# A fused encoder layer on one core: when the second block of each MLP pass adds its first tile, and what the down product of the last 32 rows waits for

## The chip, the core and the metric

The kernel runs on one core of a Trainium2 chip. A core has TensorE (matrix products), VectorE, ScalarE and GpSimd (work on whole tiles), and SyncE, which here issues most transfers. Each engine works through its own list of instructions in order, and they meet only at semaphores. The metric is the device time of one execution in microseconds, the median of three runs. In profile lines PE is TensorE, PEld its loading of weights, DVE is VectorE, ACT ScalarE, POOL GpSimd, SP or SPq SyncE's queue.

## The reference, cut to what matters

One layer of a streaming encoder: a mixer (mLSTM heads and windowed attention), an MLP, and a gated per-layer embedding with a final norm. It is computed for 2048 prompt rows and for 32 sample rows, all in float32 with a width of 1024. The change touches only the MLP:

```
x = x + jnp.square(jax.nn.relu(_rmsnorm(x, g_mlp) @ w_up)) @ w_down
```

with w_up of 1024 x 4096 and w_down of 4096 x 1024.

## The kernel before, in words

**Stages.** The mixer's work fills the first 950 us or so of the span. The MLP follows in three passes over the rows, and then the embedding's stage. The rows are 16 tiles of 128 (numbers 0 to 15) and a last one of 32 rows (number 16, called `NT`). The first pass has six tiles, the second five, the third six: the 32 last rows, and then tiles 11, 12, 15, 13, 14, in this order.

**Blocks.** Each pass goes through 16 blocks of hidden columns (`BLOCKS`), 256 columns a block. In block b TensorE first makes the up product, as seven products of half size in the manner of Strassen (`up`, L2238), and then the down product of the block before (`down(p, b - 1)`, L2291). The first block of a pass has no down product, the second has its first, and in the last block of the third pass the down products of block 14 and of block 15 come one behind the other, with the turning of the next stage's first tile between them ("drained" in `body` of `tensor`). Block 0, block 1 and the last block are written out; blocks 2 to 14 are a loop (`blocks`, L1906).

**High and low parts.** A float32 product is made of three products of rounded values (`split_product`, L107): every operand is split into a high part, made by ScalarE, and a low part, made by VectorE from the operand and its high part. For the up weights of a block there are seven such pairs: `up_weight_hi` (L2073) and `up_weight_lo` (L2367). Four of the seven weights are sums of quarters of the raw weights. `add_weights` (L2359) makes three of these sums on VectorE once the block's raw weights have landed, a fourth one stands behind the first low part (L2374). ScalarE's first high part needs the third sum. For the down weights there are two pairs (`down_weight_hi`, L2084, `down_weight_lo`, L2376).

**The down product.** `down` takes one tile after another into two accumulation banks in turn (`down_ps[n % 2]`; in the profile `m_turned` for even n and `m_proj` for odd n). A tile of 128 rows is 12 matmuls of 512 columns. Tile n waits until tile n - 2 has been added to the rows' running sum, which VectorE does in `add` (L2425, L2439), and the first two tiles wait for the low parts of the down weights. The 32 last rows are another case: their product is taken from the raw weights and an unsplit operand (L2305, 4 float32 matmuls, which the profile shows as 8), in four quarters of the bank's rows; their first add in a pass is a copy (L2431). They are the first tile (n = 0) of the third pass, and before their product TensorE waited for the two high parts of the down weights.

**VectorE's order in a block.** In blocks 1 to 14 it makes, in `body` of `vector` from L2564 on: the two low parts of the down weights (in block 1 they are made between the steps of `chain`), the combining and squaring of the seven products (`chain`, L2441), then `add_weights` for the next block, and then the adds, with the low parts of the next block's up weights between them. How many stand behind which add is said by `shared`: four of the seven in front of the middle of the tiles, the other three behind it. In the first two passes that is two behind the first add and two behind the second; in the third pass it is two, one and one.

**ScalarE's order.** In a block: its copy of the first product, the two high parts of the down weights, four high parts of the next block's up weights, two quarters of the hidden values, three more high parts, two more quarters (L2205 to L2213).

**SyncE's order.** The raw up weights of the block after next are asked for when all seven low parts of the next block are made (L1995), the raw down weights after their low parts are made and, in the third pass, after the last rows' product of the block before is done (L2000 to L2004).

Of the kernel before, what the change touches and what calls it, by code (L numbers as in the profile page):

```python
# [46 lines left out]
def reached(eng, sem, count):  # L47

    if isinstance(count, int) and count <= 0:
        return  # L50
    eng.wait_ge(sem, count)
# [1599 lines left out]
def mlp_programs(nc, ctx, m, a, x_mid, hx_kept, up_kept, w_up, w_down, x_mlp):  # L1651
# [59 lines left out]
    def tiles(p):  # L1711
        pairs = [unit for unit in UNITS[p] if len(unit) == 2]
        halved = [unit[0] for unit in UNITS[p] if len(unit) == 1]
        return [i for i in halved if i == NT] + [a for a, _ in pairs] + [i for i in halved if i != NT] + [b for _, b in pairs]

    def side0_done(p):
        return len(tiles(p)) - 1 - sum(len(unit) == 2 for unit in UNITS[p])
# [23 lines left out]
    def block_count(p, b):  # L1741
        return b + p * BLOCKS

    def made_count(p, b):
        return b + p * (BLOCKS - 1)
# [472 lines left out]
    def tensor(pe, rest):  # L2218
# [72 lines left out]
        def down(p, b):  # L2291
            k = last_group(p, b)
            w_hi, w_lo = down_hi, down_lo
            u_high, u_rest = u_split(p, b)
            for n, i in enumerate(tiles(p)):
                if i == NT:
                    reached(pe, u_hi, u_count(p, k) + 4)
                    reached(pe, down_hi_made, block_count(p, b) * 2 + 2)
                else:
                    reached(pe, u_lo, u_count(p, k) + (2 if place(p, i)[1] == 0 else 4))  # L2300
                reached(pe, added, added_count(p, b, n - 2 if n >= 2 else -1))
                if i == NT:
                    for piece in range(4):
                        f, c = piece // 2, piece % 2
                        ins = pe.matmul(down_ps[n % 2][piece * DEC:(piece + 1) * DEC, 0:NB], u_dec[:, f, :],  # L2305
                                        down_raw[:, f, c * NB:(c + 1) * NB], start=True, stop=True)
                    ins.then_inc(down_done, 1)
                    continue
                for f in (0, 1):
                    if n < 2:  # L2310
                        reached(pe, down_lo_made, block_count(p, b) * 2 + 1 + f)
                    for c in range(D // NB):
                        cols = slice(c * NB, (c + 1) * NB)
                        ins = split_product(pe, down_ps[n % 2][0:tokens(i), cols],
                                            (lambda f: stationary(u_high, f, p, i), lambda f: stationary(u_rest, f, p, i)),
                                            (lambda f: w_hi[:, f, cols], lambda f: w_lo[:, f, cols]), [f], f == 0, f == 1)
                ins.then_inc(down_done, 1)
# [19 lines left out]
    def vector(dve, rest, then):  # L2337
# [21 lines left out]
        def add_weights(g):  # L2359
            a11, a21, a22 = up_raw[:, 0, 0:HC], up_raw[:, 1, 0:HC], up_raw[:, 1, HC:KC]  # L2360
            reached(dve, up_in, g * 32 + 32)
            dve.tensor_tensor(sums_sb[:, 0], a21, a22, ALU.add).then_inc(sums, 1)
            dve.tensor_tensor(a21, a11, a21, ALU.subtract).then_inc(sums, 1)
            reached(dve, sums, g * 4 + 1)
            dve.tensor_tensor(sums_sb[:, 1], sums_sb[:, 0], a11, ALU.subtract).then_inc(sums, 1)  # L2365
# [59 lines left out]
        def add(p, b, n, i):  # L2425
            reached(dve, down_done, down_count(p, b, n))
            if i == NT:
                total, new = acc[:, n, 0:NB], down_ps[n % 2][:, 0:NB]
                if is_block(b, 0):
                    dve.wait_ge(acc_out, 16 * sum(len(tiles(m)) for m in range(p)))  # L2430
                    dve.tensor_copy(total, new).then_inc(added, 1)  # L2431
                    return
            else:
                total, new = acc[0:tokens(i), n, :], down_ps[n % 2][0:tokens(i), :]
                if is_block(b, 0):
                    dve.wait_ge(acc_in, acc_loaded(p))
            if not is_block(b, 0):
                reached(dve, added, added_count(p, b - 1, n))
            dve.tensor_tensor(total, total, new, ALU.add).then_inc(added, 1)  # L2439
# [100 lines left out]
        for p in PASSES:  # L2540
            def body(b):
                first, last = is_block(b, 0), is_block(b, BLOCKS - 1)
                if first and p == 0:
                    k, cols = group_count(p, b), all_cols(p)
                    ahead = second(p)
                    chain(k, cols.stop - cols.start, ahead)
                    for _ in range(3):
                        next(ahead)
                    for n in range(4):
                        u_low(p, b, k, cols, n)  # L2550
                    whole(ahead)
                    return
                if first:
                    for u, cols in enumerate(groups(p, b)):
                        k, w = group_count(p, b) + u, cols.stop - cols.start
                        ahead = second(p)
                        chain(k, w, ahead)
                        for _ in range(3):
                            next(ahead)
                        for n in range(4):  # L2560
                            u_low(p, b, k, cols, n)
                        whole(ahead)
                    return
                k, cols = group_count(p, b), all_cols(p)  # L2564
                if not is_block(b, 1):
                    for f in (0, 1):
                        down_weight_lo(p, b - 1, f)
                chain(k, cols.stop - cols.start, last_down_lo(p, b) if drains(p, b) else first_down_lo(p) if is_block(b, 1) else iter(()))
                if drains(p, b):
                    ahead, made = ready_pass(p + 1), 0  # L2570
                    for n, i in enumerate(tiles(p)):
                        for _ in range(lows_before(n) - made):
                            next(ahead, None)
                        made = lows_before(n)
                        u_tile_lo(p, k, n, i)
                        if n:
                            for _ in range(2):
                                next(ahead, None)
                            made += 2
                            add_drained(p, n - 1, tiles(p)[n - 1])  # L2580
                    whole(ahead)
                    add_drained(p, n, i)
                    yield
                    return
                if last:
                    for n, i in enumerate(tiles(p)):
                        add(p, b - 1, n, i)
                        if n == 0:
                            for m in range(4):
                                u_low(p, b, k, cols, m)  # L2590
                        for _ in range(ITEMS_BEFORE[n]):
                            next(then)
                    for f in (0, 1):
                        down_weight_lo(p, b, f)
                    for n, i in enumerate(tiles(p)):
                        add(p, b, n, i)
                        for _ in range(ITEMS_BESIDE[n]):
                            next(then, None)
                    whole(then)
                    yield  # L2600
                    return
                add_weights(made_count(p, b) + 1)
                ahead = ready(p, b + 1)
                half, count = side0_done(p), len(tiles(p))
                for n, i in enumerate(tiles(p)):
                    add(p, b - 1, n, i)
                    if n < half:
                        items = shared(4, half, n)
                    elif n > half:
                        items = shared(3, count - 1 - half, n - half - 1)  # L2610
                    else:
                        items = 0
                        for m in (0, 1):
                            u_low(p, b, k, cols, m)
                    for _ in range(items):
                        next(ahead, None)
                for m in (2, 3):
                    u_low(p, b, k, cols, m)
                yield

            whole(blocks(dve, p, body))
# [439 lines left out]
```

## Time and profile before

| | |
|---|---|
| time, median of 3 runs | 2599.46 us (2599.33 to 2600.07) |
| the profiled execution's own time | 2600.81 us |
| its span, first to last instruction | 2599.2 us |
| TensorE busy | 2558.8 us, 98% |
| VectorE busy | 1884.8 us, 73% |
| ScalarE busy | 905.1 us, 35% |
| mean granted TensorE clock | 0.996 |
| second block of the three passes, its down product | from 1012, 1503 and 1922 us |
| last two down products of the MLP | from 2320 and 2337 us |

Busy shares are means over the whole span; what a wait is worth is read at its place. In the rows below a line has the start, the duration, the engine, the line of the kernel, the operation, what is written and what is read, and in square brackets the idle time of the engine before it and whose work ended it. Matmuls overlap: the next one starts about 0.23 us after the one before, while a single one is shown with 0.39 us.

### The profile page before, as it was taken

To read this page: it belongs to the slowest core of one execution; us is meant where nothing else is said; L and a number is where in the kernel's file an instruction comes from. 1 tells how busy PE (TensorE), PEld (TensorE's weight loads), DVE (VectorE), ACT (ScalarE), POOL (GpSimd) and SP (SyncE) were. 2 spreads that over 40 slices of the span, in tenths; PEclk is the share of its full clock that TensorE was granted. 3 is DMA by queue.
4 is the path that set the end of the run, shared out by engine and by line. 5 is a ranking of instruction groups with operands and counts; after the bars stand their busy time and mean duration, and the time that the engine had idled before them with its cause. 6 is when DMAs were issued, how large, how long until landed. Compare 5 with 4: busy or idle time off the path is not lost.

```text
span 2599.2 us, 40780 instructions
## 1 busy us (share of the span) xinstructions
PE 2558.8 (98%) x14143; PEld 2224.1 (86%) x14143; DVE 1884.8 (73%) x3281; ACT 905.1 (35%) x2097; POOL 78.7 (3%) x170
## 2 busy tenths in 40 slices
PE   8999999999999999999999999999999999999999
PEld 6888888878888878999999888989888888888887
DVE  7777777775555568777777788888887887885443
ACT  5333333454444443222222323232332332343322
POOL 0000000000000000000000000000000000000010
PEclk9999999999999999999999999999999999999999
DMA  5112111542232336222222542323342222233223
GB/s 211 58 57 85 56 56 51 178 156 98 105 109 97 112 129 236 65 65 65 65 65 65 196 136 65 97 65 97 121 156 81 65 80 65 81 142 135 86 73 108
DMA packets 163367, 261.86 MB, mean 101 GB/s; under 512 B 11440, under 2 KB 111256, under 8 KB 162520
## 3 DMA queue, kind: packets, MB, share of 16 engines
q1 hardware_dynamic: 160936, 252.29, 28.9%
q0 software_dynamic: 2352, 8.52, 1.0%
q8 instruction: 49, 0.80, 0.1%
q14 instruction: 30, 0.25, 0.0%
HBM read 199.99 MB, written 60.62 MB: 100 GB/s over the span
## 4 chain that ended last, share of the span: by engine, by line
PE 89%; DVE 6%; issue 2%; ACT 1%; DMA 1%; POOL 0%; ACTq 0%; DVEq 0%; SPq 0%; POOLq 0%
PE m_proj L112 12%; PE m_proj L114 12%; PE m_proj L113 12%; PE m_turned L112 6%; PE m_turned L114 6%; PE m_turned L113 6%; PE m_acc L114 5%; PE m_acc L112 5%; PE m_acc L113 5%; PE m_pair L113 4%; PE m_pair L112 4%; PE m_pair L114 4%; PE m_pair L1260 1%; PE m_turned L1268 1%; PE m_acc L1285 1%
## 5 line engine op out<-in xcount | busy, mean ns | idle before, releaser
L2082 ACT ACTIVATE f_up_hi<-f_sums 128x512 fp32r<-128x512 f32 x138 | 85.8, 621 | 507.1 <-DVE f_sums L2365 489.8
L2396 DVE TENSOR_TENSOR f_part<-f_part,m_acc 128x384 f32<-128x384 f32 (+2 forms) x240 | 119.2, 513 | 139.9 <-PE m_acc L114 137.1
L112 PE MATMUL m_proj<-f_down_hi,f_uT_hi 128*128 128x512 f32 x476 | 188.9, 397 | 2.5 <-DVE f_acc L2439 2.5
L114 PE MATMUL m_proj<-f_down_hi,f_uT_lo 128*128 128x512 f32 x476 | 185.6, 390 | 0.0
L112 PE MATMUL m_turned<-f_down_hi,f_uT_hi 128*128 128x512 f32 x472 | 183.9, 390 | 1.6 <-DVE f_acc L2431 0.9
L113 PE MATMUL m_proj<-f_down_lo,f_uT_hi 128*128 128x512 f32 x476 | 185.2, 389 | 0.0
L113 PE MATMUL m_turned<-f_down_lo,f_uT_hi 128*128 128x512 f32 x472 | 184.1, 390 | 0.0
L114 PE MATMUL m_turned<-f_down_hi,f_uT_lo 128*128 128x512 f32 x472 | 183.9, 390 | 0.0
L2439 DVE TENSOR_TENSOR f_acc<-f_acc,m_proj 128x1024 f32<-128x1024 f32 x118 | 143.7, 1218 | 45.4 <-PE m_proj L114 45.2
L2439 DVE TENSOR_TENSOR f_acc<-f_acc,m_turned 128x1024 f32<-128x1024 f32 x131 | 151.5, 1156 | 27.6 <-PE m_turned L114 25.5
L2106 ACT ACTIVATE f_uT_hi<-f_part 128x256 fp32r<-128x256 f32 (+2 forms) x300 | 92.3, 364 | 202.0 <-PE m_turned L114 122.2
L2372 DVE TENSOR_TENSOR f_up_lo<-f_up_raw,f_up_hi 128x512 fp32r<-128x512 f32 x184 | 123.2, 683 | 0.0
L112 PEld LDWEIGHTS m_proj<-f_down_hi,f_uT_hi 128*128 128x128 f32 x476 | 89.3, 188 | 38.8 <-issue 13.5
L2378 DVE TENSOR_TENSOR f_down_lo<-f_down_raw,f_down_hi 128x1024 fp32r<-128x1024 f32 x92 | 108.3, 1214 | 0.0
L114 PEld LDWEIGHTS m_proj<-f_down_hi,f_uT_lo 128*128 128x128 f32 x476 | 89.3, 188 | 19.2
L112 PEld LDWEIGHTS m_turned<-f_down_hi,f_uT_hi 128*128 128x128 f32 x472 | 88.6, 188 | 20.0 <-issue 2.4
L2082 ACT ACTIVATE f_up_hi<-f_up_raw 128x512 fp32r<-128x512 f32 x184 | 104.7, 616 | 0.0
L113 PEld LDWEIGHTS m_proj<-f_down_lo,f_uT_hi 128*128 128x128 f32 x476 | 89.4, 188 | 17.8
L114 PEld LDWEIGHTS m_turned<-f_down_hi,f_uT_lo 128*128 128x128 f32 x472 | 88.6, 188 | 18.6
L113 PEld LDWEIGHTS m_turned<-f_down_lo,f_uT_hi 128*128 128x128 f32 x472 | 88.6, 188 | 17.5
L112 PE MATMUL m_proj<-a_wo_hi,a_mixT_hi 128*128 128x512 f32 x256 | 103.1, 403 | 0.0
L2400 DVE SCALAR_TENSOR_TENSOR f_part<-f_part 128x384 f32<-128x384 f32 (+2 forms) x192 | 99.4, 518 | 5.0
(452 smaller groups left out, 7324.8 us busy)
## 6 DMA issues: line engine op xcount, KB each, us to landing
f_down_raw<-in_w_down SPq DMA_DIRECT2D x96, 512.0 KB, 5.1
f_up_raw<-in_w_up SPq DMA_DIRECT2D x92, 512.0 KB, 5.2
hT_hi_kept<-m_hT_hi SPq DMA_DIRECT2D x17, 512.0 KB, 5.0
hT_lo_kept<-m_hT_lo SPq DMA_DIRECT2D x17, 512.0 KB, 5.8
a_hT_hi<-hT_hi_kept SPq DMA_DIRECT2D x17, 512.0 KB, 3.7
a_hT_lo<-hT_lo_kept SPq DMA_DIRECT2D x17, 512.0 KB, 4.6
m_x<-in_x_prompt SPq DMA_DIRECT2D x16, 512.0 KB, 4.2
a_x_sum<-in_x_prompt SPq DMA_DIRECT2D x16, 512.0 KB, 6.2
```

The costliest lines, as they stand in the source:

```text
L112: eng.matmul(out, lh(k), rh(k), start=f, stop=False)
L113: eng.matmul(out, lh(k), rl(k), start=False, stop=False)
L114: ins = eng.matmul(out, ll(k), rh(k), start=False, stop=e)
L1260: ins = pe.matmul(out, head, kT[:, g, 0:slots, :], start=n == 0, stop=n == 1)
L1268: ins = pe.transpose(turned[0:n, p * GRP + h, 0:t.n], s[0:t.n, g, h, p * P:p * P + n], ident[0:t.n, 0:t.n])
L2082: act.activation(up_hi[:, q], weight(q), ACT.Copy).then_inc(up_hi_made, 1)
L2106: ins = act.activation(out, part[PART_OF[quarter]][:, at], ACT.Copy)
L2372: dve.tensor_tensor(up_lo[:, q], weight(q), up_hi[:, q], ALU.subtract).then_inc(up_lo_made, 1)
L2378: dve.tensor_tensor(down_lo[:, f], down_raw[:, f], down_hi[:, f], ALU.subtract).then_inc(down_lo_made, 1)
L2396: dve.tensor_tensor(part[out][:, 0:w], part[other][:, 0:w], up_ps[bank][:, 0:w], ALU.add).then_inc(combined, 1)
L2400: dve.scalar_tensor_tensor(x, x, 0.0, x, ALU.max, ALU.mult).then_inc(squared, 1)
L2439: dve.tensor_tensor(total, total, new, ALU.add).then_inc(added, 1)
```

## The change

Two edits. In the second block of a pass (`is_block(b, 1)`), `add_weights` is called behind the first add instead of ahead of all adds. In the other blocks it stays ahead of them. In `down`, the product of the 32 last rows waits on the two semaphores that count the arrivals of the raw down weights, instead of on the one that counts their high parts.

```
@@ def down(p, b)
             for n, i in enumerate(tiles(p)):
                 if i == NT:
                     reached(pe, u_hi, u_count(p, k) + 4)
-                    reached(pe, down_hi_made, block_count(p, b) * 2 + 2)
+                    for f in (0, 1):
+                        reached(pe, down_in[f], block_count(p, b) * 16 + 16)
                 else:
@@ def vector(dve, rest, then)
-                add_weights(made_count(p, b) + 1)
                 ahead = ready(p, b + 1)
                 half, count = side0_done(p), len(tiles(p))
+                if not is_block(b, 1):
+                    add_weights(made_count(p, b) + 1)
                 for n, i in enumerate(tiles(p)):
                     add(p, b - 1, n, i)
+                    if n == 0 and is_block(b, 1):
+                        add_weights(made_count(p, b) + 1)
                     if n < half:
                         items = shared(4, half, n)
```

## Rows read from the trace of the kernel before

**Rows 1.** The page, part 1: busy us, share of the span, instructions of each engine.
```profile
PE 2558.8 (98%) x14143; PEld 2224.1 (86%) x14143; DVE 1884.8 (73%) x3281; ACT 905.1 (35%) x2097; POOL 78.7 (3%) x170
```
**Rows 2.** Waits of PE, 1010 to 2362: total us, times, longest.
```profile
PE m_proj L112 <- DVE f_acc L2439: 2.5, 14, 0.2
```
**Rows 3.** Timeline of PE, second pass, second block, first to fourth tile.
```profile
1505.92 0.39 PE L114 MATMUL m_turned<-f_down_hi,f_uT_lo 128*128 128x512 f32 x1
...
1509.70 0.47 PE L112 MATMUL m_turned<-f_down_hi,f_uT_hi 128*128 128x512 f32 x1 [0.67 <-DVE f_acc L2439]
...
1512.64 0.47 PE L112 MATMUL m_proj<-f_down_hi,f_uT_hi 128*128 128x512 f32 x1
```
**Rows 4.** Timeline of PE, third pass, second block: last rows, third and fourth tile.
```profile
1922.66 1.07 PE L2305 MATMUL m_turned<-f_down_raw,f_u_dec 128*32 128x512 f32 x8
...
1927.57 0.47 PE L112 MATMUL m_turned<-f_down_hi,f_uT_hi 128*128 128x512 f32 x1 [0.89 <-DVE f_acc L2431]
...
1930.74 0.47 PE L112 MATMUL m_proj<-f_down_hi,f_uT_hi 128*128 128x512 f32 x1 [0.19 <-DVE f_acc L2439]
```
**Rows 5.** Timeline of PE, first pass, second block: first tile's end, third, fourth.
```profile
1014.54 0.39 PE L114 MATMUL m_turned<-f_down_hi,f_uT_lo 128*128 128x512 f32 x1
...
1017.49 0.39 PE L112 MATMUL m_turned<-f_down_hi,f_uT_hi 128*128 128x512 f32 x1
...
1020.21 0.39 PE L112 MATMUL m_proj<-f_down_hi,f_uT_hi 128*128 128x512 f32 x1
```
**Rows 6.** Timeline of PE, end of the MLP, around the last rows' last product.
```profile
2334.43 0.39 PE L114 MATMUL m_proj<-f_down_hi,f_uT_lo 128*128 128x512 f32 x1
...
2337.02 1.07 PE L2305 MATMUL m_turned<-f_down_raw,f_u_dec 128*32 128x512 f32 x8 [1.11 <-ACT f_down_hi L2087]
2338.02 0.50 PE L112 MATMUL m_proj<-f_down_hi,f_uT_hi_last 128*128 128x512 f32 x1
```
**Rows 7.** Timeline of DVE, third pass, first block: first low behind its sums.
```profile
1907.76 0.69 DVE L2372 TENSOR_TENSOR f_up_lo<-f_sums,f_up_hi 128x512 fp32r<-128x512 f32 x1 [0.75 <-ACT f_up_hi L2082]
```
**Rows 8.** Timeline of DVE, end of the MLP.
```profile
2334.86 1.22 DVE L2439 TENSOR_TENSOR f_acc<-f_acc,m_proj 128x1024 f32<-128x1024 f32 x1 [0.37 <-PE m_proj L114]
2336.01 2.36 DVE L2378 TENSOR_TENSOR f_down_lo<-f_down_raw,f_down_hi 128x1024 fp32r<-128x1024 f32 x2
```
**Rows 9.** Timeline of DVE, first pass, second block.
```profile
1014.99 0.68 DVE L2365 TENSOR_TENSOR f_sums<-f_sums,f_up_raw 128x512 f32<-128x512 f32 x1
1015.59 1.21 DVE L2439 TENSOR_TENSOR f_acc<-f_acc,m_turned 128x1024 f32<-128x1024 f32 x1
1016.72 0.68 DVE L2372 TENSOR_TENSOR f_up_lo<-f_sums,f_up_hi 128x512 fp32r<-128x512 f32 x1
...
1018.53 1.21 DVE L2439 TENSOR_TENSOR f_acc<-f_acc,m_proj 128x1024 f32<-128x1024 f32 x1
```
**Rows 10.** Timeline of DVE, second pass, second block.
```profile
1506.53 0.69 DVE L2362 TENSOR_TENSOR f_sums<-f_up_raw 128x512 f32<-128x512 f32 x1 [0.54 <-DMA f_up_raw<-in_w_up]
...
1508.35 1.21 DVE L2439 TENSOR_TENSOR f_acc<-f_acc,m_turned 128x1024 f32<-128x1024 f32 x1
```
**Rows 11.** Timeline of DVE, third pass, second block.
```profile
1924.94 0.68 DVE L2362 TENSOR_TENSOR f_sums<-f_up_raw 128x512 f32<-128x512 f32 x1
...
1926.74 0.68 DVE L2431 COPY f_acc<-m_turned 128x512 f32<-128x512 f32 x1
...
1929.39 1.21 DVE L2439 TENSOR_TENSOR f_acc<-f_acc,m_proj 128x1024 f32<-128x1024 f32 x1
```
**Rows 12.** Timeline of PE, third pass, inside the loop: up's end, last rows' product.
```profile
1951.81 0.31 PE L114 MATMUL m_acc<-f_2op,f_up_lo 128*128 128x336 f32 x1
1952.05 1.07 PE L2305 MATMUL m_turned<-f_down_raw,f_u_dec 128*32 128x512 f32 x8
```
**Rows 13.** Timeline of PE and windows (busy by engine, PEclk, DMA, GB/s) behind a wait.
```profile
979.67 0.41 PE L2231 MATMUL m_pair<-f_op,f_up_hi 128*128 128x384 f32 x1 [1.97 <-ACT f_op L2134]
...
980.00:985.00 5.00, 5.00 (x31) 5.00 (x30) 5.00 (x10) 3.70 (x8) 0.00 (x0) 1.00 0.95 299
```

More of the change, by code:

```diff
@@ L2297, in down @@
                     reached(pe, u_hi, u_count(p, k) + 4)
-                    reached(pe, down_hi_made, block_count(p, b) * 2 + 2)
+                    for f in (0, 1):
+                        reached(pe, down_in[f], block_count(p, b) * 16 + 16)
                 else:
@@ L2601, in body @@
                     return
-                add_weights(made_count(p, b) + 1)
                 ahead = ready(p, b + 1)
                 half, count = side0_done(p), len(tiles(p))
+                if not is_block(b, 1):
+                    add_weights(made_count(p, b) + 1)
                 for n, i in enumerate(tiles(p)):
                     add(p, b - 1, n, i)
+                    if n == 0 and is_block(b, 1):
+                        add_weights(made_count(p, b) + 1)
                     if n < half:
```

## The prediction, made before the changed kernel was run

> **What bounds the kernel now.** The page's busy times come first: TensorE works 98% of the span [rows 1], so only two things can move the end, the work on TensorE and its idle time. The change alters no matmul. What is left is the list of TensorE's waits, read from the stretch of the MLP (1010 to 2362 us), and after it the timelines around each place that the diff touches. The reader is to see there that TensorE hardly waits inside a block: its commonest wait is that of the down product of the fourth tile for the second add, 14 times at most 0.2 us [rows 2]. The places where the first tile's add comes late are two single waits, 0.67 us in the second pass [rows 3] and 0.89 us in the third [rows 4], and one stall of 1.11 us stands ahead of the last rows' product at the MLP's end [rows 6]. The first pass has none there [rows 5]. These are the prizes; all three together are 2.7 us, 0.1% of the time.
>
> **What the order is.** In a down stage TensorE makes one tile after another into two banks in turn, 12 matmuls and 2.72 us a tile (1017.49 to 1020.21, [rows 5]). The third tile needs the first tile's add, the fourth the second's, and so on. On VectorE the second block has, after its squares: three sums, add 1, low of weight 0 with a fourth sum, low of weight 1, add 2. The change makes it add 1, three sums, and the rest. No instruction is added or dropped there; none of the moved ones issues a DMA. But two things are new: the sums now stand behind a wait for TensorE's first tile, and the whole path from the sums through ScalarE's first high part to the first low now stands between add 1 and add 2. Before, add 1 itself filled the time in which ScalarE made the high part. With nothing in between, VectorE idles 0.75 us at that handover [rows 7], so from the start of the third sum to the start of the first low it is 0.69 + 0.75 = 1.44 us.
>
> **First pass.** The first tile's last matmul starts at 1014.54 and ends at 1014.93 [rows 5]. An add that waits for TensorE follows the last matmul's end by 0.04 us (2334.43 + 0.39 = 2334.82 to 2334.86, [rows 6, 8]), so add 1 starts at 1014.97 instead of 1015.59. The step to the next instruction is 1.13 us (1015.59 to 1016.72, [rows 9]), a sum's is 0.60 (1014.99 to 1015.59, [rows 9]). Sums start at 1016.10, 1016.70 and 1017.30; first low 1018.74; fourth sum 1019.34; second low 1019.94; add 2 at 1020.54, ended 1021.75. Before, it started at 1018.53 [rows 9]. TensorE takes up 0.14 us after an add's end (1508.35 + 1.21 = 1509.56 to 1509.70, [rows 3, 10]): the fourth tile starts at 1021.89, against 1020.21 in a row of matmuls without a gap [rows 5]. That is 1.68 us, and 0.08 for the first matmul after a wait (0.47 against 0.39 us, [rows 3, 5]): **+1.76 us** where nothing was to be won. Add 3 then starts at 1022.87 (two lows behind add 2) and ends 1024.1, before TensorE is through with the fourth tile (1024.7), so the delay does not grow.
>
> **Second pass.** Tile 1 ends at 1505.92 + 0.39 = 1506.31 [rows 3]; add 1 starts at 1506.35, the sums at 1507.48, 1508.08 and 1508.68 (the transfer that they waited for landed by 1506.53, [rows 10], so that wait is gone). First low 1510.12, add 2 at 1511.92, ended 1513.13, fourth tile at 1513.27 against 1512.64 [rows 3]: **+0.63 us**. The 0.67 us wait of the third tile does go, and TensorE gives it back, and more, one tile later.
>
> **Third pass.** Here the first tile is the 32 last rows, whose sum is a copy of 0.68 us [rows 11] and whose product is done at 1923.7 [rows 4], so the copy takes the slot of the first sum, 1924.94 [rows 11]. Sums 1925.54, 1926.14, 1926.74; first low 1928.18; fourth sum, second low; add 2 at 1929.98 against 1929.39 [rows 11], ended 1931.19, fourth tile 1931.33 against 1930.74 [rows 4]: **+0.59 us**. The 0.89 us ahead of the third tile go and come back.
>
> **Last rows' product.** It asks for two arrivals of the raw weights instead of ScalarE's two high parts. In 15 of its 16 calls the high parts are made long before, so nothing moves: the list of waits names this line once, with the wait of the last call [rows 6]. In the last call it waited for them until 2337.02 [rows 6]. What then ends last is the add of the tile before: started 2334.86, ended 2336.07 [rows 8], taken up at 2336.21. The eight matmuls occupy TensorE for 1.00 us (2337.02 to 2338.02, [rows 6]), to 2337.21. The next tile needs the first low of the down weights, which starts at 2336.01 [rows 8] and at 1.21 us ends at 2337.22, taken up 2337.36. It started at 2338.02: **−0.66 us**, not 1.11, since the low parts are late next. I followed the adds behind it: each ends 0.5 us or more before the tile that wants it, so the 0.66 us are kept.
>
> **The added wait.** 16 calls have one wait more on TensorE's queue. The trace has no pair with and without one. Start to start, the last up matmul and the first of the last rows' product are 0.24 us apart inside the loop [rows 12]; the up matmuls themselves are 0.15 apart. So three waits and the other shape cost 0.09 us together, at most 0.03 each: 0 to 0.5 us for 16, and below nothing there is nothing, since a wait gives no time back. I take 0, because TensorE's queue runs ahead of the array when the waits are already met. A rule speaks against this: the Trainium skill, Advanced Engine Details and Errata, section Network/Comms, gives 50 to 100 ns for a sequencer's reading of a semaphore. By that 16 waits would be an estimate of 0.8 to 1.6 us; the trace has three waits in 0.09 us, so it disagrees unless the queue hides them.
>
> **The sum.** 1.76 + 0.63 + 0.59 − 0.66 = +2.32 us. Everything behind each place is TensorE without gaps, so shifts are passed on whole. The profiled execution took 2600.81 us over a span of 2599.2; its like after the change would have 2603.1 and 2601.5. It lies 1.35 us above the median of the runs, 2599.46, and what is added is the same for both: **2601.8 us**, 0.09% more.
>
> **Rivals.**
> - *The early add pays (faster).* If add 2 is not late, because VectorE gets from add 1 to add 2 as quickly as before, the two waits of the third tile (0.83 and 1.04 us with their slow first matmul) are simply gone, and with 0.66 us the time is 2597.0. For it: those waits exist. Against: it decides at add 2 ending by 1020.07 in the first pass, while the work between needs it until 1021.75; ScalarE would have to begin on the high parts before the sums exist. Chance 6%.
> - *The added wait costs.* Each of the 16 calls loses 0.05 to 0.1 us more: half a microsecond by my upper bound, 2602.3; with three times that 2603.4. For it: the calls are on the full engine's own queue. Against: [rows 12]. Chance 12%.
> - *TensorE's clock falls in the new gap.* The new waits leave TensorE idle for 1.5 to 1.9 us (in the third pass from 1929.4, where its third tile now ends, to 1931.33). If the granted clock went to the lower of its two levels (1.2 of 2.4 GHz) for a tile, 12 matmuls of 0.227 us would take twice as long: +2.7 us, 2604.5. Against: after an idle time of 1.97 us the granted clock in the next 5 us was 1.00 [rows 13]. The Trainium skill, TensorE: Matmul & The Clock Gate, Part 1, says that the throttled state is the default and activity releases it; by that rule a gap is a danger, and the trace shows none of this length that did harm. Chance 2%.
> - *Only the last product's part works* and the order on VectorE is harmless (a second add that TensorE needs later than I read): 2598.8. Chance 5%.
>
> **Chances and range.** Forecast 75%. A measurement of this kernel tells 0.2%, 5.2 us, from no change; every case but an unknown one lies inside. Faster 0.02, same 0.95, slower 0.03 (the clock with the added wait). The range for 8 in 10 takes the forecast, the runs' spread (0.7 us), the bound of the added wait and part of its rival: 2600.6 to 2603.4. The fast cases stay outside.
>
> **What would show it.** Right: VectorE's second-block order add, three sums, 0.75 us idle, low; add 2 some 2 us later in the first pass; in TensorE's list of waits three waits of the fourth tile, some 1.5, 1.5 and 1.9 us long, in place of 0.67 and 0.89 of the third; last rows' product started right behind an add, and a wait of 0.1 us at the tile behind it. Wrong: a fourth tile in the first pass that starts without a gap; 15 larger gaps ahead of the last rows' product; a granted clock below 1.00 in the tiles behind a new wait.

## The result, and the profile after

The changed kernel took 2603.02 us (median of 20 runs, 2601.25 to 2605.45) against 2598.89 us of the kernel before (20 runs, 2597.09 to 2601.17): ratio 1.0017, interval 1.001 to 1.0024, so 4.1 us or 0.17% slower. The forecast was 2601.8 us and 2.3 us more. The direction and the place were right; the size was short by 1.8 us, and most of that is one mechanism, a fall of TensorE's clock, to which the prediction had given 2 chances in 100. The forecast of the time itself came nearer (1.2 us short) than that of the difference, and that is luck: the three runs that it started from lay 0.6 us above the median of the twenty.

The list of TensorE's waits in the MLP stretch of the changed kernel (engine, line, who is waited for: us in total, times, longest) is the first thing to read:

```profile
PE m_proj L112 <- DVE f_acc L2440: 7.6, 16, 1.9
PE m_pair L112 <- DVE f_2op L2347: 1.0, 1, 1.0
PE m_acc L112 <- DVE f_up_lo L2373: 0.4, 1, 0.4
PE m_turned L2306 <- DVE f_acc L2440: 0.3, 1, 0.3
```

The waits of the third tile have gone, and the line of the fourth tile has grown from 2.5 us in 14 waits [rows 2] to 7.6 in 16. Of the 1.11 us ahead of the last rows' product [rows 6], 0.3 are left.

VectorE's timeline of the changed kernel, first pass, second block (start, us, line, operation):

```profile
1013.04 1.22 DVE L2440 TENSOR_TENSOR f_acc<-f_acc,m_turned 128x1024 f32<-128x1024 f32 x1 [1.09 <-PE m_turned L114]
1014.18 0.68 DVE L2363 TENSOR_TENSOR f_sums<-f_up_raw 128x512 f32<-128x512 f32 x1
...
1015.38 0.68 DVE L2366 TENSOR_TENSOR f_sums<-f_sums,f_up_raw 128x512 f32<-128x512 f32 x1
1016.82 0.69 DVE L2373 TENSOR_TENSOR f_up_lo<-f_sums,f_up_hi 128x512 fp32r<-128x512 f32 x1 [0.75 <-ACT f_up_hi L2082]
...
1018.63 1.22 DVE L2440 TENSOR_TENSOR f_acc<-f_acc,m_proj 128x1024 f32<-128x1024 f32 x1
```

From the start of add 1 to the start of add 2 it is now 5.59 us; before it was 2.94 [rows 9]. VectorE idles twice here: 1.09 us ahead of add 1, until TensorE's first tile is done, and 0.75 us between the two adds, for ScalarE's first high part.

TensorE's timeline of the changed kernel at the same place, the fourth tile:

```profile
1019.99 0.47 PE L112 MATMUL m_proj<-f_down_hi,f_uT_hi 128*128 128x512 f32 x1 [1.55 <-DVE f_acc L2440]
```

And in the second pass, the fourth tile in full to the first matmul of the fifth. Read the starts: they should be 0.23 us apart.

```profile
1513.47 0.47 PE L112 MATMUL m_proj<-f_down_hi,f_uT_hi 128*128 128x512 f32 x1 [1.82 <-DVE f_acc L2440]
1513.78 0.51 PE L113 MATMUL m_proj<-f_down_lo,f_uT_hi 128*128 128x512 f32 x1
1514.09 0.63 PE L114 MATMUL m_proj<-f_down_hi,f_uT_lo 128*128 128x512 f32 x1
1514.51 0.63 PE L112 MATMUL m_proj<-f_down_hi,f_uT_hi 128*128 128x512 f32 x1
...
1516.65 0.63 PE L114 MATMUL m_proj<-f_down_hi,f_uT_lo 128*128 128x512 f32 x1
1517.07 0.51 PE L112 MATMUL m_proj<-f_down_hi,f_uT_hi 128*128 128x512 f32 x1
...
1517.87 0.39 PE L112 MATMUL m_turned<-f_down_hi,f_uT_hi 128*128 128x512 f32 x1
```

From 1514.09 on they are 0.43 us apart, for some 3 us. The windows of the same execution (busy us and instructions by engine, then the granted clock, the DMA share, GB/s) show why. The second line is the third pass's; its fourth tile had a wait of 1.94 us ahead of it, and its clock stayed at 1.00:

```profile
1513.00:1518.00 5.00, 4.53 (x13) 3.62 (x14) 3.60 (x8) 1.32 (x3) 0.00 (x0) 0.66 0.00 0
1933.00:1938.00 5.00, 4.25 (x19) 3.56 (x20) 4.18 (x6) 1.18 (x7) 0.00 (x0) 1.00 0.00 0
```

In the second pass the granted clock behind the wait fell to the lower of its two levels (1.2 GHz) for some 3 us and came back. I call this a dip. TensorE had been idle for 1.8 us before it. The tile took 4.40 us where the fourth tile behind a wait takes 2.81 (third pass, 1930.74 to 1933.55 in the timeline before): 1.6 us.

The end of the MLP in the changed kernel:

```profile
2339.30 1.06 PE L2306 MATMUL m_turned<-f_down_raw,f_u_dec 128*32 128x512 f32 x8 [0.31 <-DVE f_acc L2440]
2340.45 0.47 PE L112 MATMUL m_proj<-f_down_hi,f_uT_hi_last 128*128 128x512 f32 x1
```

**The account by starts of tiles.** Whole spans of single executions mislead here: the profiled one of the changed kernel is 2601.4 us, only 2.2 above the 2599.2 of before. The MLP's first down product began at 1012.01 in the profile before and at 1010.08 in this one, ahead of any edited instruction. The window from 910 to 960 us shows where the 1.9 us are, first before, then after:

```profile
910.00:960.00 50.00, 47.81 (x260) 37.86 (x259) 28.76 (x56) 22.46 (x66) 3.86 (x8) 0.97 0.37 121
```
```profile
910.00:960.00 50.00, 47.81 (x268) 37.95 (x267) 30.35 (x58) 23.33 (x67) 3.85 (x8) 1.00 0.37 121
```

In all 14 profiles of this study the clock there was either 1.00, with the MLP beginning at 1009.5 to 1011.1, or 0.97, with a beginning at 1011.5 to 1012.4. The profile before was one of the latter. So I compare each edited place from a start ahead of it to one behind it. First pass, second tile to the next up product: 13.60 us before (1014.77 to 1028.37), 15.39 after (1012.84 to 1028.23), +1.79. Second pass: 12.03 (1506.15 to 1518.18), 14.54 (1506.05 to 1520.59), +2.51. Third pass, from the last rows' product: 16.33 (1922.66 to 1938.99), 16.93 (1925.07 to 1942.00), +0.60. End, from the next stage's turning to its first product: 17.32 (2334.66 to 2351.98), 16.66 (2337.73 to 2354.39), −0.66. The sum is +4.24, for an execution with one dip, and the medians say +4.1.

### The profile page after: what moved, and what is told of

It reads as the page before. It is cut to its first block, busy times and chain, and to the rows that moved or that the text cites. A ratio compares the mean times of both kernels' runs of the same rounds, so it can differ in the third digit from the quotient of the medians.

```text
span 2601.4 us, 40809 instructions
## 1 busy us (share of the span) xinstructions
PE 2558.2 (98%) x14143; PEld 2223.5 (85%) x14143; DVE 1884.9 (72%) x3281; ACT 904.9 (35%) x2097; POOL 78.7 (3%) x170
## 4 chain that ended last, share of the span: by engine, by line
PE 89%; DVE 7%; issue 2%; ACT 1%; DMA 1%; POOL 0%; ACTq 0%; DVEq 0%; SPq 0%; POOLq 0%
PE m_proj L112 12%; PE m_proj L114 12%; PE m_proj L113 12%; PE m_turned L113 6%; PE m_turned L112 6%; PE m_turned L114 6%; PE m_acc L114 5%; PE m_acc L112 5%; PE m_acc L113 5%; PE m_pair L112 4%; PE m_pair L113 4%; PE m_pair L114 4%; PE m_pair L1260 1%; PE m_turned L1268 1%; PE m_acc L1285 1%
```

## The experiments

Theory T: the second add comes late, and the longer of the waits that this makes let TensorE's clock fall, in some executions. Timed runs are given against the kernel before on the same chip. "By the stretches" means the sum of the four differences of the account above, taken from one profile.

**The order alone (order_only).**

```
-                    for f in (0, 1):
-                        reached(pe, down_in[f], block_count(p, b) * 16 + 16)
+                    reached(pe, down_hi_made, block_count(p, b) * 2 + 2)
```

> The first edit alone (the early add in the second block of each pass), the last rows' product waiting for the high parts as before. Theory T (the second add comes late, and the wait that this makes in the second pass lets TensorE's clock fall): waits of the fourth tile of about 1.55, 1.8 and 1.9 us; local costs +1.8, +0.9 to +2.5 (the larger with a granted clock well under 1 in the stretch of some 4 us behind it) and +0.6 us, so +4.8 us over the kernel before. Rival R1 (the result lies higher than the sum of steps because of the second edit's added wait on TensorE's queue): +3.0 us here, and the clock dip is a chance event seen in one execution.

Measured 2603.97 against 2598.61 us, ratio 1.0021 (1.0012 to 1.003): +5.4 us, where R1 had +3.0. Waits of 1.55, 1.83 and 1.96 us. Its dip was behind the third of them, not the second:

```profile
1513.00:1518.00 5.00, 4.57 (x20) 3.81 (x21) 5.00 (x10) 1.27 (x3) 0.00 (x0) 1.00 0.00 0
1933.00:1938.00 5.00, 5.00 (x17) 3.96 (x16) 2.58 (x4) 1.17 (x7) 0.00 (x0) 0.66 0.00 0
```

So the dip is no fixed cost of one pass: each of the two waits can have it or not. Without it the second pass costs 12.99 − 12.03 = +0.96 us (1506.00 to 1518.99).

**The wait alone (wait_only).** The change's second edit (the last rows' product waits for the raw weights) on its own, on the kernel before.

> The second edit alone (the last rows' product waits for the raw weights), all adds and sums in the old order. Theory T: TensorE's wait of 1.11 us at the last call becomes one of 0.3 us plus 0.15 us at the tile behind it, -0.65 us in the whole, and the gap ahead of the other 15 calls stays 0.24 us start to start. Rival R1 (the added wait costs): gaps of 0.3 us or more ahead of the calls in the loop, +0.8 to +1.6 us in the whole.

Measured 2598.58 against 2598.61 us, ratio 0.9999 (0.999 to 1.0009): the times alone can't tell 0.65 us from nothing. The trace can: the last rows' product waited 0.31 us, and from the turning to the next product it is 16.65 us (2334.95 to 2351.60) instead of 17.32. Ahead of the other calls the step stayed at 0.24 to 0.25 us, here inside the loop of the changed kernel (compare [rows 12]):

```profile
1954.82 0.31 PE L114 MATMUL m_acc<-f_2op,f_up_lo 128*128 128x336 f32 x1
1955.06 1.06 PE L2306 MATMUL m_turned<-f_down_raw,f_u_dec 128*32 128x512 f32 x8
```

From the product in block 1's place to that in block 14's (13 calls on) it was 367.86 us before and 367.92 after. In order_only, which has no added wait, it is 367.90 (1955.07 to 2322.97). The added wait costs at most 0.06 us in 13 calls. R1 falls.

**Matmuls in the gap (fill).**

```
+                if n == 3 and is_block(b, 0):
+                    reached(pe, combined, group_count(p, b + 1) * 7 + 7)
+                    for _ in range(6):
+                        pe.matmul(up_ps[B], stationary(uT_hi, 0, p, i), down_hi[:, 0, 0:NB], start=True, stop=True)
                 reached(pe, added, ...)
```

> The changed kernel with six matmuls of 128x128 by 128x512 more, written to a bank that nobody reads, just ahead of the fourth tile's wait in the second block of each pass (their product is not used). They take 6 x 0.23 = 1.4 us of the 1.5 to 1.9 us in which TensorE idled. Theory T (the idle time makes the clock fall): granted clock 1.00 behind the wait in the second pass, the fourth tile 2.8 us instead of 4.4, about 1.6 us less than the changed kernel: +2.6 us over the kernel before. Rival R2 (the clock dip has nothing to do with this idle time): the dip stays or falls elsewhere, and the time is that of the changed kernel, +4.2 us.

Measured 2601.93 against 2598.61 us, ratio 1.0012 (1.0002 to 1.0021): +3.3 us, between the two, nearer to T. In the trace the fourth tile starts as late as in the changed kernel (16.95 us for the third pass's stretch, against 16.93), but it takes 2.90 us in the second and third passes, and the clock stays:

```profile
1513.00:1518.00 5.00, 4.62 (x21) 3.62 (x20) 5.00 (x10) 1.55 (x3) 0.00 (x0) 1.00 0.00 0
1932.00:1937.00 5.00, 4.49 (x20) 3.68 (x20) 4.18 (x6) 1.29 (x7) 0.00 (x0) 1.00 0.01 3
```

By the stretches it costs 1.77 + 0.92 + 0.62 − 0.65 = +2.66 us. It is one profile, and single waits of the changed kernel stay without a dip too, so the trace alone would not settle it. The times help: in the same comparison the unfilled kernel (the next run) took 2603.52 us, 1.6 us more, as T had it.

**The changed kernel again (after_again, and two single executions with a profile, after_third and after_fourth).**

> The changed kernel once more. Theory T: waits of the fourth tile of 1.55, 1.8 and 1.9 us as in its first profile, and the clock dip behind the second of them again, at the same tile; +4.2 us. Rival R2 (a chance event): no dip, or one behind another wait; then the time of most executions would be +2.6 us.

> The changed kernel, one more profile, to count the dips. Theory T: waits of 1.55, 1.83 and 1.95 us; no dip in the first pass, one behind at least one of the other two.

> The changed kernel, one more profile, to count the dips. As for the one before: none in the first pass, one at least in the other two.

Measured for the first 2603.52 against 2598.61 us, ratio 1.0017 (1.0008 to 1.0026). Its waits were 1.55, 1.83 and 1.95 us, and it had two dips, in the second and the third pass:

```profile
1513.00:1518.00 5.00, 4.91 (x15) 3.94 (x16) 3.52 (x8) 0.94 (x2) 0.00 (x0) 0.66 0.01 3
1933.00:1938.00 5.00, 4.61 (x13) 3.68 (x14) 2.58 (x4) 0.00 (x0) 0.00 (x0) 0.66 0.00 0
```

The two single profiles had one each, both in the third pass. With the first profile that is 5 dips behind 8 waits of 1.8 us or more in four executions of the changed kernel, and none behind its four waits of 1.55 us. So R2 was right that chance has a part in it, and wrong that most executions go without: this run's median is 4.9 us above the kernel before, not 2.6.

**A longer wait in the first pass (long_gap, and a second profile, long_gap_2).**

```
                     if n < half:
                         items = shared(4, half, n)
+                        if p == 0 and is_block(b, 1):
+                            items = (3, 1)[n]
```

> The changed kernel with one low (0.6 us) moved from behind add 2 to ahead of it in the second block of the first pass only: TensorE's wait there grows from 1.55 to 2.15 us. Theory T (a wait of 1.8 us or more lets the clock fall in most executions, one of 1.55 us does not): a dip behind it with 4.4 us for the fourth tile, more often than not, so +0.6 us and +1 us on average over the changed kernel. Rival R5 (the dips belong to the place, not to the length of the wait): none in the first pass, +0.6 us.

> The kernel with 2.15 us of wait in the first pass once more, one profile. Theory T (length decides, by chance of the moment): a dip in the first pass is likelier than not. Rival R5 (the place decides): none there again.

Measured 2605.24 us (7 runs) against 2598.52, ratio 1.0026 (1.0015 to 1.0037): +6.7 us. The first profile had no dip in the first pass, and one in the second: as R5 would have it. The second had one in the first pass, behind a wait of 2.15 us, and its fourth tile took 4.42 us:

```profile
1018.00:1022.00 4.00, 2.34 (x11) 1.60 (x9) 3.29 (x5) 3.76 (x8) 0.00 (x0) 1.00 0.01 2
1022.00:1027.00 5.00, 4.52 (x13) 3.62 (x14) 3.01 (x5) 0.93 (x2) 0.00 (x0) 0.66 0.02 3
```

That rules R5 out for the MLP as "never in the first pass". "More often than not" is not shown by one in two.

**Shorter waits everywhere (short_gap).**

```
+                        if is_block(b, 1):
+                            items = ((1, 3), (1, 3), (1, 2, 1))[p][n]
```

> The changed kernel with one low (0.6 us) moved from ahead of add 2 to behind it in the second block of all three passes. Theory T (late by so many lows, and the clock falls only behind the longer waits): waits of the fourth tile of 0.95, 1.2 and 1.35 us, no dip of the clock in any pass, local costs +1.2, +0.3 and 0 us and -0.65 at the end: +0.9 us over the kernel before. Rival R5 (the dips belong to the place): the same waits, but fourth tiles of 4.4 us in the second or third pass, +2.5 us or more.

Measured 2600.30 against 2598.68 us, ratio 1.0007 (0.9998 to 1.0016): +1.6 us, which the interval does not tell from nothing. Waits of 0.94, 1.23 and 1.37 us, as worked out from the lows' 0.6 us, and no dip:

```profile
1020.00:1024.00 4.00, 3.24 (x13) 2.47 (x14) 4.00 (x7) 2.42 (x5) 0.00 (x0) 1.00 0.01 2
1513.00:1518.00 5.00, 4.16 (x17) 3.22 (x18) 5.00 (x10) 2.29 (x7) 0.00 (x0) 1.00 0.00 0
1932.00:1937.00 5.00, 4.79 (x21) 3.98 (x22) 4.75 (x9) 1.68 (x8) 0.00 (x0) 1.00 0.00 0
```

By the stretches it costs 1.41 + 0.58 + 0.07 − 0.65 = +1.4 us and not the +0.9 expected: the lows moved behind add 2 make add 3 late, and the fifth tile of the first pass starts 2.94 us behind the fourth, where 2.80 is what a tile behind a wait takes.

**No early add in the first pass (not_first).**

```
-                if not is_block(b, 1):
+                if not is_block(b, 1) or p == 0:
                     add_weights(made_count(p, b) + 1)
...
-                    if n == 0 and is_block(b, 1):
+                    if n == 0 and is_block(b, 1) and p:
```

> The changed kernel without its early add in the first pass (the second and third passes keep it). Theory T: the first pass gives back its 1.8 us, no wait there; the second and third cost +0.9 and +0.6 us and the dips as before: +2.5 us or so over the kernel before on average. Rival R6 (part of the first pass's delay was taken up later by slack): as the changed kernel, +4 us or a little less.

Measured 2603.04 against 2598.52 us, ratio 1.0015 (1.0006 to 1.0024): +4.5 us, a miss, and no clear step down from the changed kernel. The trace has the first pass's stretch back at 13.62 us, so its 1.8 us did go, against R6; this execution had two dips (2.55 us more in the second pass, 2.27 in the third), and so comes to +4.2 by its stretches. Its eleven times fall in two groups, four from 2600.7 to 2601.3 and seven from 2603.0 to 2604.9. My +2.5 took fewer dips than seven of the runs seem to have had; whether a dip is likelier in this kernel than in the changed one stays open.

**Both adds where they fit (two_adds, two_adds_all).** In the second block add 2 goes where VectorE idled for ScalarE; two_adds_all has also the two lines with `PASSES[-1]`, which move one low from ahead of add 2 to behind it in the third pass's other blocks.

```
-                    if n < half:
+                    if is_block(b, 1) and n < 3:
+                        items = 2 * min(n, 1)
+                        if n == half:
+                            for _ in range(items):
+                                next(ahead, None)
+                            items = 0
+                            for m in (0, 1):
+                                u_low(p, b, k, cols, m)
+                    elif n < half and p == PASSES[-1]:
+                        items = [1, 2, 1][n]
+                    elif n < half:
                         items = shared(4, half, n)
```

> The changed kernel with another order in the second block of each pass: add 1, the three sums, add 2, low of weight 0 with the fourth sum, low of weight 1, add 3, the other two lows, and on as before. Add 2 falls into the time in which ScalarE makes the first high part. Theory T (what costs is the second add's lateness): no wait of the third or the fourth tile in any pass; by the tiles' starts -1.1 us in the second pass, -1.5 us in the third, 0 in the first, -0.65 us at the end, no clock dip, -3.3 us against the kernel before. Rival R3 (the sums, asked for later than before, delay ScalarE's high parts and through them the next block's up products): waits for low parts at the start of block 2's up products, and a time no better than before.

> As the run before, and in blocks 2 to 14 of the third pass the lows stand 1, 2, 1 behind the first three adds instead of 2, 1, 1, so add 2 is one low (0.6 us) earlier. Theory T: the wait of the fourth tile there (0.17 us, and 0.4 us of time each by the starts of the tiles in block 2) goes in all 13 blocks, -5 us more, -8.5 us against the kernel before. Rival R4 (that wait only moves to the tile behind it, since VectorE is the bound of the third pass): -3.3 us as in the run before.

Measured for two_adds 2595.52 against 2598.52 us, ratio 0.9989 (0.998 to 0.9998). VectorE in its first pass, where the idle 0.75 us has gone:

```profile
1017.57 0.68 DVE L2366 TENSOR_TENSOR f_sums<-f_sums,f_up_raw 128x512 f32<-128x512 f32 x1
1018.17 1.21 DVE L2440 TENSOR_TENSOR f_acc<-f_acc,m_proj 128x1024 f32<-128x1024 f32 x1
1019.30 0.68 DVE L2373 TENSOR_TENSOR f_up_lo<-f_sums,f_up_hi 128x512 fp32r<-128x512 f32 x1
```

Its stretches are 13.64, 10.88 and 14.74 us: +0.04, −1.15 and −1.59, no wait and no dip in them. For two_adds_all 2590.77 us (5 runs) against 2598.52, ratio 0.9965 (0.9951 to 0.9978), and the line of the fourth tile is missing from the list of waits:

```profile
PE m_pair L112 <- DVE f_2op L2347: 1.0, 1, 1.0
PE m_acc L112 <- DVE f_up_lo L2373: 0.4, 1, 0.4
PE m_turned L2306 <- DVE f_acc L2440: 0.3, 1, 0.3
```

From block 2's up product to the last rows' product of block 15 in the third pass it is 374.55 us (1936.24 to 2310.79) instead of 380.92 (1938.99 to 2319.91): 0.49 us for each of 13 blocks. R3 and R4 fall. It beats both kernels. By the stretches and these 13 blocks it gains 9.7 us, and the two profiled executions, which both begin the MLP at 1012 us, differ by 10.0 (2590.78 against 2600.81); the medians differ by only 7.7, where 8.5 was forecast. With five runs that gap stays open.

## Why the prediction was right, and where its size was short

- **First pass** (+1.76): measured +1.79. The step "add 2 at 5.6 us behind add 1" came out at 5.59.
- **Second pass** (+0.63): measured +2.51 in the first profile, +0.92 in after_third, which had no dip there (1505.53 to 1518.48). Two steps of it failed. The first is the handover: I took 0.75 us of idle from the third pass's first block [rows 7], but at this place ScalarE starts 0.37 us behind the sum and not 0.08, and VectorE idled 1.03 us. The trace of before had it, hidden under add 1: ScalarE started at 1508.79 behind a sum that ended at 1508.43. I took a row from another stage where the place had its own. What ScalarE waits for there the profile does not name. The second step is the clock. ScalarE's high part before the change, then VectorE's first low after it:

```profile
1508.79 0.63 ACT L2082 ACTIVATE f_up_hi<-f_sums 128x512 fp32r<-128x512 f32 x1 [9.00 <-issue]
```
```profile
1510.30 0.69 DVE L2373 TENSOR_TENSOR f_up_lo<-f_sums,f_up_hi 128x512 fp32r<-128x512 f32 x1 [1.03 <-ACT f_up_hi L2082]
```

- **Third pass** (+0.59): measured +0.60 without a dip. With one, 18.57 us for the stretch in after_third, +2.24.
- **Last rows' product** (−0.66): −0.66. The low parts were next, as said.
- **The added wait** (0): 0.06 us in 13 calls at most. The 50 to 100 ns that the Trainium skill gives in Advanced Engine Details and Errata, section Network/Comms, do not show on TensorE's queue here.
- **The clock** (a rival, 2 in 100, +2.7 us for a tile): this is the term that was mis-sized. It cost 1.6 us a time and not 2.7, since the clock came back after some 3 us, and it came far more often than 2 times in 100: in the eight profiles whose second and third passes had waits of 1.82 to 1.97 us, a dip followed 10 of 16 of them. With 5 dips in 4 executions of the changed kernel the expected cost is 1.79 + 0.92 + 0.60 − 0.66 + 1.25 x 1.6 = +4.65 us; measured were +4.1 and +4.9. I had excluded it on one row, a wait of 1.97 us at the end of the mixer with a clock of 1.00 behind it [rows 13], and wrote that no gap of this length in the trace had done harm. That reading was wrong. The same trace has a wait of 1.89 us 32 us earlier, with the clock low behind it:

```profile
947.63 0.55 PE L1274 MATMUL m_turned<-m_ident,a_hx 128*128 128x128 f32 x3 [1.89 <-DVE a_mixT_lo L1390]
948.00:953.00 5.00, 5.00 (x24) 4.29 (x23) 3.04 (x8) 1.12 (x3) 0.00 (x0) 0.66 0.38 134
```

The changed kernel's first profile has the same wait, and no dip:

```profile
947.79 0.44 PE L1274 MATMUL m_turned<-m_ident,a_hx 128*128 128x128 f32 x2 [1.90 <-DVE a_mixT_lo L1390]
948.00:953.00 5.00, 5.00 (x37) 4.11 (x35) 4.16 (x10) 1.29 (x4) 0.00 (x0) 1.00 0.41 143
```

From this wait to the next one it is 16.38 us with the dip and 14.78 without: the 1.6 us of the MLP's dips, to be read before anything was changed. The Trainium skill says in TensorE: Matmul & The Clock Gate, Part 1, that the throttled state is the default and activity releases it. The traces agree with this: the clock fell behind idle time and was back at 1.00 some 3 us after the work had begun again. The prediction set that rule aside too cheaply.

- **The rival that the early add pays** failed as said: the wait moved one tile on, and grew. (Its 2597.0 us is a slip: 2599.46 − 0.83 − 1.04 − 0.66 is 2596.9.)

What is shown: the wait moved and what it costs; that in the MLP dips follow the waits of 1.8 us and more in any pass, none the eight of 1.55 us and less (five in the first pass of kernels with the early add, three in short_gap), and none the filled gaps. What is not: that the length of a wait decides. Outside the MLP it does not. Two places of the mixer, which no edit touches, have the same wait in all 14 profiles, 1.65 us at about 520 us and 1.89 or 1.90 us at about 948. In seven profiles the clock fell behind both, in the other seven behind neither, so the shorter wait brings dips too, and the two places are not independent of each other. At the place of [rows 13] the twelve waits of 1.40 to 2.11 us had none, and the two of 2.86 and 2.94 us both had one. What decides whether a given wait brings a dip stays open.

## What to carry to other kernels

An operation moved ahead to end one wait takes what stood before it along as a delay for the next: follow the queue to the second and third consumer before counting the gain. The place for it is where the engine idles anyway; here that was one add further on, and the same two adds in the right slots gave 3.0 us where the change lost 4.1. A wait on TensorE near 2 us should be priced with a clock dip as a chance, not left out because one row went well. Look for all waits of that length in the trace at hand, and read the clock behind each.

## What the runs showed of the hardware that I had not expected

The granted clock falls to 1.2 GHz behind an idle stretch of 1.65 to 2.2 us in some executions and not in others of the same kernel. In the MLP, and behind the waits of 1.65 and 1.89 us in the mixer, it was low for some 3 us at a cost of 1.6 us each time. The mixer is untouched by the change: with a dip behind its wait of 1.89 us the window 910 to 960 us has a clock of 0.97 and not 1.00, and the MLP begins some 2 us later. This is a good part of the 4 us by which executions of one kernel differ, and it hid half of the difference between the two profiled spans.
